# Queries and keys of two attentions projected with tokens on partitions and turned by DMA, memory values with a column of ones, and an earlier start of the first merge

## What is computed

```python
x = x + 0.5 * swiglu_ffn(rms_norm(x, g_ffn1), w_ffn1_in, w_ffn1_out)
h = rms_norm(x, g_mix)
rq, rk, rv, rg, dq, dk, dv, mq, gates = split(h @ w_in)
# A: retention, 4 heads of 256 (values 512)
ret = rms_norm(retention(rq, rk, rv, positions)) * silu(rg)
# B: causal differential attention, 8 heads, 2 maps of width 64, values 128
dqn = rms_norm(dq.reshape(B, S, 8, 2, 64), g_diff_q)
dkn = rms_norm(dk.reshape(B, S, 8, 2, 64), g_diff_k)
dif = rms_norm(diff_attention(dqn, dkn, dv, lam), g_diff_out) * (1 - lam_init)
# C: attention over 256 memory tokens, 4 heads of 256
mk, mv = split(rms_norm(mem, g_mem) @ w_mem_kv)
mo = softmax(rms_norm(mq, g_mem_q) @ rms_norm(mk, g_mem_k).T / 16) @ mv
y = sig(g0) * (ret @ w_br_ret) + sig(g1) * (dif @ w_br_diff) + sig(g2) * (mo @ w_br_mem)
x = x + y @ w_o
x = x + 0.5 * swiglu_ffn(rms_norm(x, g_ffn2), w_ffn2_in, w_ffn2_out)
```

## Time and profile before

| | |
|---|---|
| median of 3 runs | 2389.83 us (2389.46 to 2392.04) |
| the profiled execution's own time | 2388.88 us |
| its span on the slowest core (core 2) | 2387.8 us (the others 2382.2 to 2387.5) |
| mean granted TensorE clock of the cores | 0.995 to 0.997 |
| TensorE busy | 2321.8 us, 97% |
| VectorE, ScalarE, POOL busy | 1222.9, 984.8, 149.8 us |
| chain that ended last | PE 90%, ACT 4%, DVE 2%, all else 1% or less each |

### The profile page before, as it was taken

The page is one execution under the profiler, slowest core; times in us unless marked ns, Lnnn a source line. Parts: engine busy times, 40 slices in busy tenths (PEclk is TensorE's granted clock), DMA queues, the critical chain, the costliest instruction groups (busy, mean ns, idle before and its releaser), DMA issues.

```text
span 2387.8 us, 34149 instructions; the slowest of 8 cores (2382.2 to 2387.8 us)
## 1 busy us (share of the span) xinstructions
PE 2321.8 (97%) x13284; PEld 1112.4 (47%) x13284; DVE 1222.9 (51%) x2359; ACT 984.8 (41%) x1679; POOL 149.8 (6%) x173
## 2 busy tenths in 40 slices
PE   6999999999999999999999999999999999999998
PEld 2444444444444444454444465555554444444443
DVE  5577334485565552113444576677754655344334
ACT  3111110357767764144631487788851221111110
POOL 1000000230000000000000111121100000000000
PEclk9999999999999999999999999999999999999999
DMA  8221221353442424342102200201305322321313
GB/s 232 49 50 24 52 38 34 82 135 58 67 79 37 83 43 74 54 73 51 20 16 46 46 12 10 45 13 28 48 10 141 71 45 36 53 36 24 47 18 141
DMA packets 86779, 132.69 MB, mean 56 GB/s; under 512 B 71648, under 2 KB 72032, under 8 KB 75360
## 3 DMA queue, kind: packets, MB, share of 16 engines
q0 software_dynamic: 10512, 75.50, 18.8%
q1 hardware_dynamic: 76112, 55.00, 9.1%
HBM read 172.43 MB, written 16.78 MB: 79 GB/s over the span
## 4 chain that ended last, share of the span: by engine, by line
PE 90%; ACT 4%; DVE 2%; POOL 1%; DMA 1%; issue 1%; SPq 0%; POOLq 0%; DVEq 0%; ACTq 0%
PE pw L605 90%; ACT ET L616 2%; POOL acc L628 1%; ACT nrs L616 1%; DMA stg<-w_ffn_in 1%; DMA memT<-mem 0%; ACT L616 0%; DVE dq L620 0%; DVE dU L639 0%; ACT sqf L616 0%; SPq L647 0%; DVE mqn L620 0%; DVE dn L620 0%; ACT nsq L616 0%; ACT sgt L616 0%
## 5 line engine op out<-in xcount | busy, mean ns | idle before, releaser
L605 PE MATMUL pw<-hT,wbuf 128*128 128x512 bf16 x4864 | 1168.5, 381 | 12.3 <-ACT nrs L616 5.6
L605 PEld LDWEIGHTS pw<-hT,wbuf 128*128 128x128 bf16 x4864 | 471.5, 98 | 551.9 <-issue 29.4
L616 ACT ACTIVATE sgf<-pw 128x512 f32<-128x512 f32 x176 | 104.1, 596 | 702.6 <-PE pw L605 702.5
L605 PE MATMUL pw<-uu,wbuf 128*128 128x512 bf16 x1408 | 334.1, 379 | 0.0
L605 PE MATMUL pw<-wbuf,hT 128*128 128x512 bf16 x1280 | 303.2, 379 | 0.2 <-DVE sgR L628 0.2
L616 ACT ACTIVATE ET<-pw 128x1024 bf16<-128x1024 f32 (+1 forms) x288 | 265.9, 975 | 66.9 <-PE pw L605 64.0
L628 DVE TENSOR_TENSOR uu<-pw,sgf 128x512 bf16<-128x512 f32 x176 | 120.8, 690 | 275.7 <-PE pw L605 275.5
L605 PEld LDWEIGHTS pw<-uu,wbuf 128*128 128x128 bf16 x1408 | 137.7, 98 | 166.1 <-issue 0.2
L605 PEld LDWEIGHTS pw<-wbuf,hT 128*128 128x128 bf16 x1280 | 123.0, 98 | 137.5 <-issue 0.6
L605 PE MATMUL pw<-Vd,ET 128*128 128x129 bf16 x2176 | 173.2, 220 | 8.3 <-DVE dU L639 4.5
L620 DVE SCALAR_TENSOR_TENSOR xT<-pw,xT 128x512 f32<-128x512 f32 x192 | 130.4, 688 | 78.4 <-PE pw L605 74.7
(11 more groups left out here) (120 smaller groups left out, 2153.6 us busy)
## 6 DMA issues: line engine op xcount, KB each, us to landing
wbuf<-w_in POOLq DMA_DIRECT2D x26, 1024.0 KB, 8.3
wbuf<-w_ffn_in POOLq DMA_DIRECT2D x21, 1024.0 KB, 10.3
wbuf<-w_ffn_out POOLq DMA_DIRECT2D x10, 1024.0 KB, 9.6
xs<-xT SPq DMA_DIRECT2D x4, 2048.0 KB, 11.6
xT<-x SPq DMA_DIRECT2D x6, 1024.0 KB, 22.9
wbuf<-w_br_ret POOLq DMA_DIRECT2D x4, 1024.0 KB, 8.0
wbuf<-w_mem_kv POOLq DMA_DIRECT2D x4, 1024.0 KB, 10.5
x2l<-xs SPq DMA_DIRECT2D x2, 2048.0 KB, 14.5
```

What stands on the lines that cost most here:

```text
L605: return Op("pe", lambda e: e.matmul(out, lhsT=lhsT, rhs=rhs, start=start, stop=stop, **kw), reads, writes, n / 2400.0 + 0.003, 0.17, sign ...
L616: return Op("act", lambda e: e.activation(out=out, in_=in_, func=func, **kw), reads, writes, c, 0.08, fuse=("accum_out" not in kw), tab=TA ...
```

## The change

1. **Memory queries.** `m_proj` projects with 128 tokens of h stationary and 512 weight columns (two heads) moving: per t and pair of heads, four banks of 8 matmuls. The new `m_q` squares each head's 256 columns on ACT with a running sum (`accum_out`), takes Ln and Exp of 128 x 2, scales on DVE into `nsq` and flips 128 x 512 into `mqn`.
2. **Memory values.** `mvT` gets a column of ones per head, and the value matmuls take 128 tokens of `EM` stationary and 257 columns moving. DVE takes the reciprocal of column 257, scales into `nsq`, and a flip brings the result to `MO`, whose layout changes (`m_src`). The two matmuls of ones with their Ln and Exp on 128 x 512 are gone.
3. **Differential queries and keys.** Columns of q and k of one head lie side by side in `w_in`; a bank takes two groups of 128 tokens by 256 columns (16 matmuls of 256 columns). `d_qk`: ACT squares into `nrs`, DVE multiplies by the gains into `qraw` and reduces to 128 x 8, ACT takes Ln and Exp of 128 x 8, POOL scales into `nsq`, and a flip writes `dqk`, from which the scores read q and k. The matmul with `bd64` is gone, and so is its bank.
4. **Buffers.** `nsq` has 4 tiles in place of 3 and serves all of the above; `dn` is gone, and `d_tail` uses `nsq` too. `EM` moves over `memT`.
5. **The order.** A flip is modelled to land 3.0 us after its issue (`LAND`), and the memory load 8 us later than the model had it. The first merge waits only for `Tm`. `d_v(1)` has priority 11 in place of 9, and the projections of `d_proj` are let in after `i * 3 - 3` pairs in place of `i * 4 - 4`.

```diff
         if op.dma is not None:
-            self.t_dma = max(self.t_dma, s + 0.5) + op.dma
-            fin = self.t_dma + 2.0
+            if op.dma < 1.0:
+                fin = s + op.dma + LAND
+            else:
+                ...
-        nsq = [fixed(f"nsq{i}", TT, BF16) for i in range(3)]
+        nsq = [fixed(f"nsq{i}", TT, BF16) for i in range(4)]
...
         def m_load():
             yield spdma(memT[:, :], mem_d[:, :], [], [memTb], 1 << 20)
+            memTb.w_fin += 8.0
...
+        def m_q(b, mi, c, key):
+            yield mss_s.free
+            u = mss_s.get()
+            for hh in range(2):
+                ...
+                yield act(nrs[j][:, 0:256], bk(b)[:, hh * 256:hh * 256 + 256], AF.Square, ..., accum_out=s1)
+            ...
+            ln = act(s2, s2, AF.Ln, ..., scale=1.0 / 256.0)
+            yield ln
+            yield act(s2, s2, AF.Exp, ..., scale=-0.5)
+            yield nsq_s.free
+            n = nsq_s.get()
+            for hh in range(2):
+                yield stt(nsq[n][:, sl], bk(b)[:, sl], mss[...], gmq[:, :], ALU.mult, ALU.mult, ..., 256)
+            banks_held.discard(b)
+            yield flip(mqn[mi][:, c * TT:(c + 1) * TT]..., nsq[n][:, :], [nsqb[n]], [mqnb[mi][c]], 131072)
+            nsq_s.put(n)
...
         def m_core(...):
-                yield mm(bk(m), ones1, nsq[i][:, :], dc == 0, dc == 1, ...)
-                yield mm(bk(b), ones1, EM[es_[mt]][:, :], mt == 0, mt == 1, ...)
-                    yield mm(bk(b), mvT[:, o:o + 128], EM[es_[mt]][:, :], mt == 0, mt == 1, ...)
+                        yield mm(bk(b)[:, 0:257], EM[e][:, c * 128:(c + 1) * 128], mv4[:, mt, hm, 0:257], ..., 257)
+                    yield Op("dve", lambda e, b=b, rc=rc: e.reciprocal(out=rc, in_=bk(b)[:, 256:257]), ...)
+                    yield ts(nsq[n][:, sl], bk(b)[:, 0:256], rc, None, ALU.mult, None, ..., 256)
+                yield flip(MO[:, o * TT:(o + 1) * TT]..., nsq[n][:, :], [nsqb[n]], [MOb[o]], 131072)
...
         def d_qk(...):
-            yield cp(qraw[r][:, :], bk(b), ...)
-            yield tt(nsq[i][:, :], qraw[r][:, :], qraw[r][:, :], ALU.mult, ..., eng="pool")
-            yield mm(bk(m), bd64, nsq[i][:, :], True, True, ...)
-            yield act(nrs[j][:, :], bk(m), AF.Ln, ..., TT)
-            yield act(nrs[j][:, :], nrs[j][:, :], AF.Exp, ..., TT)
-            yield stt(dst[:, t * TT:(t + 1) * TT], qraw[r][:, :], pvec[:, g:g + 1], nrs[j][:, :], ...)
+            yield act(nrs[j][:, :], bk(b), AF.Square, [bkb[b]], [nrsb[j]], TT)
+            yield tt(qraw[r]..., bk(b)..., gqk..., ALU.mult, [bkb[b], b_gqk], [qrawb[r]], TT)
+            yield Op("dve", lambda e: e.reduce_sum(out=ss, in_=nrs[j][:, :].rearrange("p (g d) -> p g d", g=8), ...))
+            yield act(ss, ss, AF.Ln, ...)
+            yield act(ss, ss, AF.Exp, ...)
+            yield tt(nsq[n]..., qraw[r]..., ss..., ALU.mult, ..., eng="pool")
+            yield flip(sl.rearrange("p (a n) -> p a n", a=4), nsq[n][:, :], [nsqb[n]], [dqkb[h % 2][i]], 131072)
...
         def d_proj():
-                    for k in range(KC):
-                        yield mm(bk(b), wt[:, o:o + 128], hs(t, k), k == 0, k == KC - 1, ..., TT)
+                    for cc in range(2):
+                        for k in range(KC):
+                            yield mm(bk(b)[:, cc * 256:cc * 256 + 256], hcol(i // 2, k, (i % 2) * 2 + cc), wt[:, o:o + 256], ..., 256)
...
-            yield lambda: ("rcore", 14) in flags and len(Tm_s.held) == 0 and len(sgt_s.held) == 0
+            yield lambda: len(Tm_s.held) == 0
```

More of the change, by code:

```diff
@@ L24 @@
 NCORES = 8
+LAND = 3.0
 SLACK = 0.15
@@ L479, in build_program @@
         b_gdo = Buf("gdo")
-        nsqb = [Buf(f"nsq{i}") for i in range(3)]
+        nsqb = [Buf(f"nsq{i}") for i in range(4)]
         nrsb = [Buf(f"nrs{i}") for i in range(2)]
+        qssb = [Buf(f"qss{i}") for i in range(4)]
+        b_gqk = Buf("gqk")
+        mssb = [Buf(f"mss{i}") for i in range(8)]
         ssqb = [Buf(f"ssq{i}") for i in range(8)]
@@ L561, in build_program @@
             mkn, mknb = L.one("mkn", 4 * 2 * 256, BF16)
-            mvT, mvTb = L.one("mvT", 2 * 1024, BF16)
-            rlm, rlmb = L.one("rlm", TT, F32)
+            mvT, mvTb = L.one("mvT", 2 * 4 * 258, BF16)
             gsm, gsmb = L.many("gsm", 2, TT, F32)
-            mqn, mqnb = L.many("mqn", 2, 2 * TT, BF16)
+            mqn, mqnb = [], []
+            for i in range(2):
+                t_, b_ = L.one(f"mqn{i}", 4 * TT, BF16, 4)
+                mqn.append(t_)
+                mqnb.append(b_)
+            gmq, gmqb = L.one("gmq", 256, F32)
+        with Lay(SB) as L:
             EM, EMb = L.many("EM", 4, TT, BF16)
         with Lay(SB) as L:
-            dq, dqb, dk, dkb = [], [], [], []
+            dqk, dqkb = [], []
             for i in range(2):
[L570 to L575, removed]
+                t_, b_ = L.one(f"dqk{i}", 2 * S, BF16, 8)
+                dqk.append(t_)
+                dqkb.append(b_)
             qraw, qrawb = L.many("qraw", 2, TT, F32)
-            dn, dnb = L.many("dn", 2, TT, BF16)
             ET, ETb = L.many("ET", 4, 1024, BF16)
@@ L1232, in m_kv @@
                                  [wb, memhb], [bkb[b]], TT)
-                    o = mt * 1024 + vb * 512
-                    yield act(mvT[:, o:o + 512], bk(b), AF.Copy, [bkb[b]], [mvTb], TT)
+                    yield act(mv4[:, mt, vb * 2:vb * 2 + 2, 0:256], bk(b).rearrange("p (h e) -> p h e", h=2), AF.Copy,
+                              [bkb[b]], [mvTb], TT)
                     mk_pool.put(b)
                 W.give(("mkv", 2 + vb))
[L1238 to L1253, removed]
-                yield stt(mqn[mi][:, dc * TT:(dc + 1) * TT], bk(bks[dc]), pvec[:, PV_GMQ + dc:PV_GMQ + dc + 1], nrs[j][:, :],
-                          ALU.mult, ALU.mult, [bkb[bks[dc]], nrsb[j], b_const], [mqnb[mi]], TT)
-                banks_held.discard(bks[dc])
-            nrs_s.put(j)
@@ L1258, in m_core @@
+        def m_core(t, hm, mi, key):
+            for c in range(4):
+                yield flag((key, c))
+            q4 = mqn[mi][:, :].rearrange("p (c a q) -> p c a q", c=4, a=4)
             es_ = []
             for mt in range(2):
+                yield EM_s.free
+                e = EM_s.get()
+                es_.append(e)
                 yield mk_pool.free
@@ L1333, in d_qk @@
[L1333 to L1340 removed]
+            yield qss_s.free
@@ L1411, in d_score @@
                     if p == 0:
-                        yield lambda: all(("dqk", h, t, c) in flags for t in range(qt // 2 + 1) for c in range(2))
+                        yield lambda: all(("dqk", h, i) in flags for i in range(qt + 1))
                 ops = []
```

211 lines of the change are left out of this document (125 added, 86 removed).

## The result

The change makes the kernel slower: median 2437.03 us of 3 runs (2431.74 to 2677.87) against 2389.83, ratio 1.0184 with a 95% interval of 1.0154 to 1.0214. The profiled execution took 2431.74 us, its slowest core (core 0) spans 2430.5 us at a mean granted clock of 0.982, the other cores 2414.7 to 2429.2.

The account below looks back on a forecast made before the run. TensorE, busy for 2321.8 of 2387.8 us, was taken as the bound. Terms -27.6 + 1.4 - 4.8 - 1.5 + 5.6 + 5 - 5 + 3 = -23.9 us gave 2366 us, range 2351 to 2381.

Parts of the forecast that it names:

- No net change: Rival, chance 0.04: 14 us lost in reordered retention beside an SP-paced memory stage would end within 0.2% of before.
- Matmuls removed and recut: TensorE in both attentions: 128 matmuls of sums removed, -27.6 us; projections and values recut to narrower matmuls, +1.4 us.
- First merge: First merge: later modelled memory load removes TensorE's 3.15 us wait and 1.7 us of half clock, -4.8 us.
- Memory attention: Memory attention: matmuls removed, values recut, old waits gone, against a start stall of +5.6 and later flip costs of +5 us.
- The start: Start of memory attention: flips land behind two loads, TensorE waits 3.9 us plus 1.7 for the clock, +5.6 us.
- the rest, +5: Rest of memory attention: half a microsecond in each of seven later passes, 1.5 us at the end; between 0 and +12.
- SP sets the pace: Rival, chance 0.18: 64 flips, held longer by loads, stretch memory attention to 105 us in place of 95; 2376 us.
- Differential attention: Differential attention: matmuls removed -13.8, of the -27.6 us; fewer TensorE waits -5, late flips at the nsq ring +3.
- TensorE's waits on `nrs` and `dq`: Differential attention: half of 9.9 us of waits goes as banks are freed sooner, -5 us, between 0 and -10.
- The ring, +3: Differential attention: a double load stops the engine filling the four nsq tiles for a few microseconds; between 0 and +12.
- the third rival: Shared nsq ring stops VectorE at about six loads in differential attention, 46 us in place of 3; 2409 us, chance 0.06.

Follow-up runs that it names:

- The best version: Changed kernel with the landing model and memory attention of before, and the very first Ln of differential attention emitted ahead of further squares; median 2368.94 us, ratio 0.9916.
- the old model: Changed kernel with the landing model of before (all DMAs on one bandwidth clock plus 2.0 us), other edits kept; median 2383.97 us, ratio 0.9976.
- without flips: Changed kernel with the landing model of before and memory attention as before, its 64 flips gone; profiled 2373.97 us, ratio 0.9938.
- the model by the rows: Run of 2368.94 us, but flips modelled to land 2.0 us after their transfer or the last load in flight, SP 1.2 us each; median 2375.61 us, ratio 0.9946.
- four tiles: Changed kernel with landing model and memory attention of before, and four bfloat16 qraw tiles in place of two in float32; nine runs, 2375.35 to 2378.11 us.

## Why the prediction was wrong

**The step that failed** is in the sum: it has no term for retention. I read "TensorE has no gap at all, though six flips for each of its units run beside it" as a property of the stage, where it was one of the order of VectorE's work; and in the rival *No net change* I named what happened ("the new landing model also reorders retention, where TensorE is busy without a gap and a new order can only lose"), but gave it 14 us and 0.04. Both were on hand. The landings of flips after 6.0 to 9.5 us contradict a model that says 3.66, and VectorE's order at the boundary of two heads has the third `rets` write ahead of `Tm`, a comparison that I made for three places and not for this. Three boundaries with a pair of loads, each with a landing some 10 us away, make 30 us of idle time, and the clock behind them 6 more; the stage lost 40 us, against a term of nothing. I also gave the slower side 0.06 in all.

**Matmuls removed and recut** (-27.6 + 1.4): right. The best version keeps 64 of the removals, 13.8 us, and the 1.2 for the recut: 2321.8 - 12.6 = 2309.2 us of busy TensorE by my prices, 2307.5 measured. With all 128 removed and the old model it is 2321.8 - 26.2 = 2295.6, and 2297.4 measured. The step of 256 columns is (6.93 - 0.16) / 62 = 0.109 us.

**First merge** (-4.8): half right. 183.4 against 183.8 to 187.5 by core with the old model, the wait on `memT` gone, and lost again in the changed kernel, whose own order brought a gap of 5.4 us.

**Memory attention** (sum of its terms: -13.8 + 0.2 - 1.5 + 5.6 + 5 = -4.5): wrong in sign. +1.3 on the median core with the old model, up to +10.8 on the slowest, +7.1 as changed. The start cost about what was predicted, 3.9 us and 1.7 of clock: 2.94 and 1.7 in the changed kernel, 5.24 and 2.7 with the old model on its slowest core. The first, and then the longest gap of the stage on the same core:

```profile
1153.69 2.37 PE L616 MATMUL pw<-mqn,mkn 128*128 128x512 bf16 x8 [2.94 <-DMA mqn<-nsq]
...
1226.48 2.65 DVE L631 SCALAR_TENSOR_TENSOR nsq<-pw,qss,gmq 128x256 bf16<-128x256 f32 x6 [7.23 <-DMA mqn<-nsq]
...
1227.98 1.44 PE L616 MATMUL pw<-wbuf,hT 128*128 128x512 bf16 x3 [6.85 <-DVE nsq L631]
```

The term that was too small is the rest, +5. On this core it was about 18: the stage's +7.1, less -15.1 for the other terms and less 4.6 for the start. It counted half a microsecond for each pass, but the loads at the end of the stage hold the flips, `nsq` and so VectorE (waits up to 7.2 us here, 8.1 with the old model). Of the rival *SP sets the pace* the occupancy was right and the consequence not quite: the order can't mend it, but it is the landing beside loads that adds the time.

**Differential attention** (-13.8 + 1.2 - 5 + 3 = -14.6): -11.9 on the median core as changed, -3.9 on the slowest, -17.0 on the median with the first Ln ahead. I hadn't seen that the first Ln would stand behind the squares (8 us with its clock and what follows). TensorE's waits on `nrs` and `dq` (-5, of 9.9) are gone, but on core 0 of the changed kernel 12.4 us on `qraw` stand in their place. The ring, +3, showed on some cores only: cores 0 and 3 take 450.9 and 450.4 us, the others 445.0 or less, since there POOL, which fills `nsq`, stands behind a late flip (core 0):

```profile
1684.46 2.04 POOL L639 TENSOR_TENSOR nsq<-qraw,qss 128x512 bf16<-128x512 f32 x2 [19.29 <-DMA DIF<-nsq]
...
1685.53 0.69 DVE L639 TENSOR_TENSOR qraw<-pw,gqk_sb 128x512 f32<-128x512 f32 x1 [8.40 <-POOL nsq L639]
...
1686.37 0.80 PE L616 MATMUL pw<-wbuf,hT 128*128 128x256 bf16 x3 [7.42 <-DVE qraw L639]
```

This is the third rival at work in the changed kernel itself, at one place of its about six loads.

## What to carry to other kernels

A planner's model is an input to every stage: after a change to it, compare the emitted order at each place where a transfer is late in the trace, in stages that the change doesn't touch too, and ask of each engine what stands behind an operation that waits for a buffer. A model of landing has to see the transfers in flight; one number fitted to a quiet stretch reads as "free" where the buffer is held longest. Seeing them is not enough for the best order: with the first Ln ahead, the old clock, which also pushes later transfers back, gave 2368.94 us and the model by the rows 2375.61. And replacing matmuls by transposes pays only where their landings have cover, and fewer of them than the queue and the ring of buffers can turn over: here it paid in differential attention and not in memory attention.

## What the hardware showed that I had not expected

Flips in a stage can make the cores part, although all run one program. Memory attention with its merge takes 212.1 us on all eight cores before and 211.4 without flips, and 209.7 to 222.9 with 64 flips. Flips alone don't do it: retention, which has them too, takes 367.4 to 367.5 us on every core with the old model. Since the slowest core counts, a median over cores flatters such a change. A change of function table costs little here: 1.28 us, and the Ln starts 0.02 us behind it (1342.30 + 1.28, then 1343.60). The Trainium skill, page "ScalarE: Activation LUTs", section "What ACT_TABLE_LOAD costs", gives about 1283 ns for the load, as measured here, and a drain of about 1380 ns with it, which no row of this place shows; the planner's 1.3 us is thus right, and it was its use of it, not the price, that put the Ln last. And a longer ring made nothing faster where the order filled it first: the wait was 4.65 us with four tiles and 4.66 with two.
